# Key values taken out of the first values of the RWKV jobs, and gate pieces moved behind the merges

## What is computed

```python
def step(S, inp):                                  # one token, state S (64x64) of each of 16 heads
    r_t, w_t, k_t, v_t, kk_t, a_t = inp
    sa = jnp.einsum('bhvk,bhk->bhv', S, -kk_t)
    S = (S * w_t[:, :, None, :] + sa[..., None] * (kk_t * a_t)[:, :, None, :]
         + v_t[..., None] * k_t[:, :, None, :])
    y = jnp.einsum('bhvk,bhk->bhv', S, r_t) if emit else None
# run forwards and backwards, first over the 256 context tokens (state only), then over the 256 own tokens
g_rwkv, g_mla = jnp.split(jax.nn.sigmoid(p_gate + P['gate_b']), N_BRANCH, axis=-1)
merged = g_rwkv * (y_rwkv @ P['w_rwkv_proj']) + g_mla * (o @ P['w_mla_proj'])
```

## Time and profile before

| | |
|---|---|
| median of 3 runs | 3978.01 us (3964.2 to 3978.38) |
| the profiled execution: time, span | 3959.27 us, 3957.5 us |
| TensorE busy in the span | 3676.5 us (93%) |
| VectorE busy | 1319.2 us (33%) |
| ScalarE busy | 534.7 us (14%) |
| GpSimd busy | 162.4 us (4%) |
| mean granted clock of TensorE | 0.946 |

### The profile page before, as it was taken

The page is one execution under the profiler, slowest core; times in us unless marked ns, Lnnn a source line. Parts: engine busy times, 40 slices in busy tenths (PEclk is TensorE's granted clock), DMA queues, the critical chain, the costliest instruction groups (busy, mean ns, idle before and its releaser), DMA issues.

```text
span 3957.5 us, 43113 instructions
## 1 busy us (share of the span) xinstructions
PE 3676.5 (93%) x18466; PEld 2909.9 (74%) x18466; DVE 1319.2 (33%) x1920; ACT 534.7 (14%) x911; POOL 162.4 (4%) x166
## 2 busy tenths in 40 slices
PE   6999989978989869998999999999899979999979
PEld 2554545547768758887888888888788858888858
DVE  2388532235466530112321222000261261070260
ACT  1000002233333210110000000000101130101120
POOL 0020000000000000000000000000050000050000
PEclk8999999988888789999999999999899979999989
DMA  8989332012321144443444444444244303344303
GB/s 334 355 351 377 117 104 71 25 48 77 78 69 43 40 180 157 149 170 128 145 153 148 148 150 155 151 150 156 88 149 149 140 21 138 116 152 146 128 32 128
DMA packets 134889, 555.70 MB, mean 140 GB/s; under 512 B 57424, under 2 KB 62800, under 8 KB 73056
## 3 DMA queue, kind: packets, MB, share of 16 engines
q1 hardware_dynamic: 119392, 449.88, 32.6%
q10 hardware_dynamic: 15344, 103.57, 6.7%
HBM read 536.10 MB, written 17.30 MB: 140 GB/s over the span
## 4 chain that ended last, share of the span: by engine, by line
PE 59%; DVE 3%; ACT 1%; issue 1%; ACTq 0%; POOLq 0%; DVEq 0%
PE ps L433 56%; PE ps L2764 1%; PE ps L2525 0%; PE ps L2772 0%; PE ps L2520 0%; PE ps L463 0%; DVE arena L2821 0%; ACT arena L2899 0%; PE ps L2506 0%; DVE arena L2977 0%; PE ps L2773 0%; DVE arena L2286 0%; DVE arena L2960 0%; DVE arena L2741 0%; DVE arena L2295 0%
## 5 line engine op out<-in xcount | busy, mean ns | idle before, releaser
L433 PE MATMUL ps<-arena,ring 128*128 128x256 f32 (+3 forms) x11200 | 2583.2, 393 | 60.1 <-ACTq L2163 22.1
L433 PEld LDWEIGHTS ps<-arena,ring 128*128 128x128 f32 (+1 forms) x11200 | 2135.7, 191 | 504.1 <-issue 212.3
L764 DVE SCALAR_TENSOR_TENSOR arena<-arena,small 128x512 f32<-128x512 f32 x240 | 194.3, 809 | 24.0 <-DVE arena L764 9.5
L2269 DVE TENSOR_TENSOR arena<-ps,arena 128x1024 f32<-128x1024 f32 x12 | 14.3, 1222 | 394.9 <-ACT arena L2255 394.9
L2644 DVE SCALAR_TENSOR_TENSOR arena<-arena,col 128x255 f32<-128x255 f32 (+29 forms) x180 | 108.2, 601 | 6.4
L568 PE MATMUL ps<-arena 128*128 128x512 f32 (+1 forms) x224 | 90.1, 550 | 5.3 <-ACT arena L629 5.3
L2388 DVE TENSOR_TENSOR arena<-ps,arena 128x1024 f32<-128x1024 f32 x11 | 13.5, 1225 | 239.2 <-PE ps L433 239.0
L1529 PE MATMUL ps<-arena 128*128 128x256 f32 x320 | 87.4, 436 | 4.9 <-ACT arena L1739 4.9
L2652 POOL TENSOR_TENSOR arena<-arena 128x1024 f32<-128x1024 f32 x2 | 4.7, 2348 | 1994.8 <-ACT arena L2593 1994.8
L1971 DVE TENSOR_TENSOR arena<-arena 64x30 f32<-64x30 f32 (+14 forms) x240 | 83.8, 349 | 8.3
L2367 ACT ACT_TABLE_LOAD x11 | 14.1, 1283 | 535.0 <-DVE arena L2401 535.0
(11 more groups left out here) (417 smaller groups left out, 3135.8 us busy)
## 6 DMA issues: line engine op xcount, KB each, us to landing
ring<-in_weights SPq DMA_DIRECT2D x398, 1024.0 KB, 4.8
arena<-in_ada_late ACTq DMA_DIRECT2D x64, 1024.0 KB, 7.9
arena<-in_gates SPq DMA_DIRECT2D x56, 256.0 KB, 3.9
arena<-in_front ACTq DMA_DIRECT2D x8, 1024.0 KB, 9.1
arena<-in_x ACTq DMA_DIRECT2D x2, 2048.0 KB, 12.8
keep_g<-arena SPq DMA_DIRECT2D x14, 256.0 KB, 2.0
arena<-keep_g ACTq DMA_DIRECT2D x1, 3584.0 KB, 23.8
arena<-in_ctx ACTq DMA_DIRECT2D x1, 2048.0 KB, 23.6
```

The lines of the kernel that those rows point to most:

```text
L433: mm = M.matmul(o, ring[:, slot, k, c0:c0 + w], rhs, start=(kc == 0), stop=(kc == ktiles * WK - 1))
L764: ins = V.scalar_tensor_tensor(part[:, b], late[:, s, k], c, part[:, b], ALU.mult, ALU.add)
L2269: V.tensor_tensor(dst[:, 4 * b:4 * b + 4], ps[:, 4 * h:4 * h + 4, 0:T], spread(c[:, 4 * b:4 * b + 4], 4, T), ALU.mult).then_inc(dve_step.s ...
```

## The change

It does four things.

1. The product with `MR` leaves the first products. `key_values(n)` does it ahead of the own products of job n+1, 16 matmuls of 128 x 64 into a bank each for x = 0 and 1; ScalarE copies them to a new tile `Gv` (behind `turn_inverse`, `key_rates` and the gate copies), and the own products wait for both copies (`g_in`). What is left of the first products is `state_values`, 8 matmuls for each x with 64 rows each. The copy of the first values leaves ScalarE: VectorE adds state value and `Gv` (`first_values`, behind `key_factors(n+1)`, ahead of `substitute(n+1, 0..15)`).
2. ScalarE's `gate_copies(n, "own")` moves behind `turn_inverse(n)` and `key_rates(n+1)`.
3. The groups of jobs 1 to 3 that stood at "own" get the spots `LATER` and bank 5. The last piece of `STEPS` moves from "fin" to a new spot "z6", inside the merge of 64. In all, jobs 1 to 3 have none of their eight pieces ahead of the own products any more; the number of pieces is the same in each job.
4. SP loads the first group of job n before the substitution of job n is ready, not behind the unpacking. The tiles of the gate copies move (with waits for their stores in ScalarE's copies and, once, in VectorE's `key_factors`).

The diff, cut to its core:

```diff
+        Gv = view(RB + 13312, 2, 512)
...
-        gate_part = view(RB + 13312, 2, 512)
+        gate_part, gate_part_late = view(3072, 2, 512), view(RB + 21792, 512)
-        STEPS, LATER = ("z5", "x5", "x5", "fin"), ("fin", "fin", "u", "u")
-        GATE_GROUPS = [(0, 4, ("own",) * 4, "own"), (0, 5, ("own",) * 4, "own"), (0, 4, STEPS, "fin"), (0, 5, LATER, "u")]
-        GATE_GROUPS += [(n, *g) for n in range(1, 4) for g in ((4, ("own",) * 4, "own"), (4, STEPS, "fin"))]
+        STEPS, LATER = ("z5", "x5", "x5", "z6"), ("fin", "fin", "u", "u")
+        GATE_GROUPS = [(0, 4, ("own",) * 4, "own"), (0, 5, ("own",) * 4, "own")]
+        GATE_GROUPS += [(n, *g) for n in range(4) for g in ((4, STEPS, "fin"), (5, LATER, "u"))]
...
             return gate_w_late[:, k - 2]
+
+        def gate_copied(i):
+
+            return gate_part[:, i % 2] if i < CTX_GROUPS else gate_part_late
...
                 sp.wait_ge(gate_out.sem, i + 1)
-                sp.dma_start(A['keep_g'][:, i * 512:(i + 1) * 512], gate_part[:, i % 2])\
+                sp.dma_start(A['keep_g'][:, i * 512:(i + 1) * 512], gate_copied(i))\
                     .then_inc(gate_stored[i % 2].sem, 16)
...
                     sp.dma_start(gate_h_late, A['keep_h'][:, 0:2048].rearrange("p (c t) -> p c t", c=RC)).then_inc(gate_h_in.sem, 16)
-                for i in gates_by(n, "own")[n == 0:] if n < 4 else gates_of(n) if n < JOBS else ():
+                first = gates_by(n, "own") + gates_by(n, "fin") if n > 0 else gates_by(0, "own")[1:]
+                for i in first if n < JOBS else ():
                     load_gates(i)
...
-                if n < 4:
+                if n == 0:
                     for i in gates_by(n, "fin"):
...
+            def key_values(n):
+                emit = n >= 4
+                for x in range(2):
+                    p.wait_ge(ev['mr_in'], mr_count(n, 4 if emit else x + 1))
+                    p.wait_ge(ev['tok_in'], 4 * n + 2)
+                    for h in range(8):
+                        mm = M.matmul(ps[:, (4 if emit else 6) + x, h * 64:(h + 1) * 64], MR[:, x, h, 0],
+                                      vtok(n, x, h), start=True, stop=True)
+                    mm.then_inc(ev['g_mm'], 1)
+
             def gate_pieces(n, spot):
...
                     mm.then_inc(ev['z6_mm'], 1)
+                gate_pieces(n, "z6")
                 for x in range(2):
...
-            def first_products(n, x):
+            def state_values(n, x):
...
                 s, hf, q, i, b = job(n)
-                if x == 0:
-                    p.wait_ge(ev['mr_in'], mr_count(n, 4 if n >= 4 else 2))
-                    if n >= 4:
-                        p.wait_ge(ev['tr_in'], 2 * (n - 4) + 2)
+                if x == 0 and n >= 4:
+                    p.wait_ge(ev['tr_in'], 2 * (n - 4) + 2)
+                elif x == 0:
+                    p.wait_ge(ev['mr_in'], mr_count(n, 2))
                 t, st = slice(x * P, x * P + P), St[:, direction(n, x)]
                 for c in range(HF):
-                    o = [ps[:, 2 * x + e, c * 64:(c + 1) * 64] for e in range(2)]
-                    for e in range(2):
-                        M.matmul(o[e], AR[64 * e:64 * e + 64, b, c, 0, t], st[64 * e:64 * e + 64, hf * HF + c],
-                                 start=True, stop=False)
-                    for e in range(2):
-                        mm = M.matmul(o[e], MR[:, x, 4 * e + c, 0], vtok(n, x, 4 * e + c), start=False, stop=True)
+                    for e in (0, 64):
+                        mm = M.matmul(ps[:, 2 * x + e // 64, c * 64:(c + 1) * 64], AR[e:e + 64, b, c, 0, t],
+                                      st[e:e + 64, hf * HF + c], start=True, stop=True)
                 mm.then_inc(ev['u0_mm'], 1)
...
                     p.wait_ge(ev['p_in'], 2 * n + 3)
+                else:
+                    p.wait_ge(ev['g_in'], 2 * n + 2)
                 t, st = slice(x * P, x * P + P), St[:, direction(n, x)]
...
                     p.wait_ge(ev['dec_in'], n + 2)
-                    gate_pieces(n, "own")
-                    if n >= 4:
-                        p.wait_ge(ev['mr_in'], mr_count(n, 4))
-                    elif gates_by(n, "own"):
+                gate_pieces(n, "own")
+                key_values(n)
+                if more:
+                    p.wait_ge(ev['g_in'], 2 * n + 2)
+                    if gates_by(n, "own"):
                         p.wait_ge(gate_out.sem, gates_by(n, "own")[-1] + 1)
                     own_products(n + 1)
-                first_products(n, 0)
+                state_values(n, 0)
                 state_reads(n, 0)
...
                 gate_pieces(n, "z5")
-                first_products(n, 1)
+                state_values(n, 1)
                 merge_32_second(n)
...
-            def first_values(n, x):
-                a.wait_ge(ev['u0_mm'], 2 * n + x + 1)
-                S.copy(U0[:, x].rearrange("p (b t) -> p b t", b=2), ps[:, 2 * x:2 * x + 2, 0:256]).then_inc(ev['u0_in'], 1)
+            def key_values(n):
+                for x in range(2):
+                    a.wait_ge(ev['g_mm'], 2 * n + x + 1)
+                    S.copy(Gv[:, x], ps[:, (4 if n >= 4 else 6) + x, :]).then_inc(ev['g_in'], 1)
...
                 px = PX[:, n % 2]
-                first_values(n, 0)
                 reads_copy(n, 0)
...
                 S.copy(W5[96:128], w5[96:128]).then_inc(ev['z5_in'], 1)
-                first_values(n, 1)
                 a.wait_ge(ev['x5_mm'], n + 1)
...
                 for i in gates_by(n, act):
-                    if i >= 2:
-                        a.wait_ge(gate_stored[i % 2].sem, 16 * (i // 2))
+                    last = i - 2 if i < CTX_GROUPS else i - 1 if i > CTX_GROUPS else -1
+                    if last >= 0:
+                        a.wait_ge(gate_stored[last % 2].sem, 16 * (last // 2 + 1))
                     a.wait_ge(piece_mm.sem, 4 * i + 4)
-                    S.copy(gate_part[:, i % 2], ps[:, GATE_GROUPS[i][1], :]).then_inc(gate_out.sem, 1)
+                    S.copy(gate_copied(i), ps[:, GATE_GROUPS[i][1], :]).then_inc(gate_out.sem, 1)
...
                     decays(n + 1)
-                    gate_copies(n, "own")
                 turn_inverse(n)
...
                     key_rates(n + 1)
+                gate_copies(n, "own")
+                key_values(n)
                 merges(n)
...
+                    if n == 5:
+                        for stored in gate_stored:
+                            v.wait_ge(stored.sem, 16 * (CTX_GROUPS // 2))
...
                         ins.then_inc(ev['subst'], 1)
+
+            def first_values(n):
+                for x in range(2):
+                    v.wait_ge(ev['u0_mm'], 2 * n + x + 1)
+                    if x == 0:
+                        v.wait_ge(ev['g_in'], 2 * n + 2)
+                    V.tensor_tensor(U0[:, x].rearrange("p (b t) -> p b t", b=2), ps[:, 2 * x:2 * x + 2, 0:256],
+                                    Gv[:, x].rearrange("p (b t) -> p b t", b=2), ALU.add).then_inc(ev['u0_in'], 1)
...
                     key_factors(n + 1)
+                first_values(n)
                 if more:
...

```

More of the change, by code:

```diff
@@ L1241, in build_program @@
         L = {n: line(f"rw_{n}") for n in (
-            "w_mm a_mm tri_mm p_mm t_mm mr_mm tr_mm z5_mm x5_mm z6_mm fin_mm u0_mm u_mm s_mm sr_mm y_mm "
+            "w_mm a_mm tri_mm p_mm t_mm mr_mm tr_mm g_mm z5_mm x5_mm z6_mm fin_mm u0_mm u_mm s_mm sr_mm y_mm "
             "sig_in a_in dec_in kd_in ab_ready kt_ready r_ready p_in pk_out pk_in subst yt_in y_out unpacked "
-            "tok_in mr_in tr_in z5_in x5_in z6_in fin_in zero5 zero6 u0_in u_in s_in sr_in y_in "
+            "tok_in mr_in tr_in g_in z5_in x5_in z6_in fin_in zero5 zero6 u0_in u_in s_in sr_in y_in "
             "v_mm v_in sq_in ss_mm root_in inv_in kkb_mm kk_in ones_in").split()}
```

## The result

The changed kernel takes 3918.2 us (median of 4 runs, 3910.1 to 3919.6) against 3977.1 for the kernel before: a ratio of 0.9855, 95% interval 0.983 to 0.988. In a later comparison it took 3922.0 against 3965.4, ratio 0.9884 (0.9869 to 0.9899). So it is 43 to 59 us faster where 27 were forecast: the direction is right, the size is off by a factor of about two. Nearer to 43, if anything: three of the four runs of before in the first comparison lay at 3976 to 3978, while its medians in the four later ones, 58 runs in all, are 3964.8 to 3967.1.

The account below looks back on a forecast made before the run. Each job was taken as a ring from VectorE's substitution through factors, own products, packing, merges and state back to VectorE. Job terms summed to -27.1 us, giving 3932, plus 18.7 to the median: 3951 us, range 3932 to 3971.

Parts of the forecast that it names:

- allowance from one execution to the median: Whole kernel: 18.7 us between profiled execution and median of the runs before, added to the forecast 3932 to give 3951.
- x = 0 product: First product for x = 0, ahead of the merge: shortening it saves 4.6 us in job 4, 2.7 in jobs 5 and 6.
- x = 1 product: First product for x = 1, behind the merge: saves 3.0 us in jobs 0 to 3, 2.75 in 5, 4.65 in 4, 6, 7.
- Part a: Jobs 1 to 3: ScalarE's turn ahead of the gate copy brings unpacking and merge 6.15 us sooner in each.
- wait of 2 to 3 us at the merge: Jobs 1 to 3: TensorE gets a new wait of 2 to 3 us at the merge for SP's unpacking.
- Part c: Jobs 1 to 3: four gate pieces moved from 'own' to behind the merges cost 7.2 us a job at full clock.
- part b: All jobs: key product leaves the first products; key values ahead of own products take 3.7 us, 7.4 at half clock.
- More than that: Rival, 0.17: filled gap warms key values and own products in jobs 4 to 6, state values cost half; -42 us, about 3937.
- Half clock in the gap: Rival, 0.20: key values and state values run at half clock behind TensorE's gap, costing 18 us, leaving -9, 3969 us.
- gap: Experiments' theory: key values fill TensorE's idle time ahead of the own products, holding the clock; filler alone 10 to 20 us faster.
- The turn buys nothing: Rival, 0.06: something else holds the unpacking in jobs 1 to 3, so 6.15 us don't come; +18, leaving -9, 3969 us.
- slower: Rival, 0.07: light gap keeps the clock low through merges and moved pieces in jobs 1 to 3; +28, 4006 us.

Follow-up runs that it names:

- e5: Kernel before with only ScalarE's copy of the 'own' gate pieces moved behind the turn and the key rates: 3947.1 us against 3965.9, ratio 0.9952.
- e3: Changed kernel with the gate pieces of jobs 1 to 3 at their old spots, ScalarE's new order kept: 3899.0 us against 3964.8, ratio 0.9836.
- r2: Second run of e3's kernel, beside the changed kernel on the same chip: 3892.7 us against 3965.4 for the kernel before, ratio 0.9817.
- r1: Changed kernel run again unaltered for a second profile: 3922.0 us against 3965.4 for the kernel before, ratio 0.9884.
- e2: Changed kernel's pieces and orders, but the kernel before's first products, state and key matmuls pair by pair: 3970.8 us against 3964.8, ratio 1.0004.
- e1: Kernel before with each first product split into state, then key matmuls, at the old place: 3941.5 us against 3964.8, ratio 0.9943.
- e6: Changed kernel with the key values behind the own products, gap ahead of them empty: 3941.6 us against 3965.9 for the kernel before, ratio 0.9936.
- e4: Kernel before with 16 unread key-value matmuls as filler ahead of the own products in jobs 0 to 6: 3964.6 us against 3964.8, ratio 0.9997.
- e7: Changed kernel's pieces and orders, first products pair by pair, unread key matmuls filling the gap: 3979.9 us against 3965.9 for the kernel before, ratio 1.0022.
- e10: Kernel before with 16 unread 128 x 256 matmuls as heavy filler ahead of the own products in jobs 0 to 3: 3974.9 us against 3967.1, ratio 1.0015.
- e9: Changed kernel with old piece spots and ScalarE's old order, only the key values left: 3915.0 us against 3965.4 for the kernel before, ratio 0.9877.

## Why the prediction was off

**The sum by its steps.** The forecast was 3951 us, the median came out at 3918.2, 33 us below. The stage gives 31 of them (58.0 us gone in the profiles, not 27.1), and the longer part ahead of it takes 9 back. Another 10.5 are the allowance from one execution to the median: 18.7 us by three runs of before, 8.2 for the changed kernel, and 6 to 8 for before by the later medians. That allowance was put on the forecast as if it were a constant of the kernel. In the stage three blocks, predicted against measured in the two profiles of the changed kernel:

| | predicted | first profile | second profile |
|---|---|---|---|
| ahead of the merge (turn, own products late, x = 0 product) | -20.0 | -35.1 | -15.4 |
| merge to merge of 64 (x = 1 product) | -28.7 | -44.7 | -44.8 |
| from the merge of 64 on (pieces) | +21.6 | +21.8 | +21.7 |
| stage | -27.1 | -58.0 | -38.6 |

**Part a, right.** e5 measures it by itself: 19 us for three jobs, predicted 18.5. In the changed kernel the merge of jobs 1 to 3 comes 13.4, 14.4 and 14.6 us after the masks in the first profile and 14.4, 14.2 and 15.6 in the second, predicted 14.6. What the earlier trace rows say of the factor and the earlier trace rows of the unpacking was read correctly. The wait of 2 to 3 us at the merge was not: it is 0.3, 0 and 1.5 us, 0, 1.1 and 2.6 in the second profile, mostly because the own products come later and at half clock.

**Part c, right.** The moved pieces cost 21.8 and 21.7 us, predicted 21.6; e3's kernel gets them back and 7 more (29 us, r2 beside r1). What I called "the change's headline part, a and c together, is worth 3 us in all" is what e2 measures: no difference. (By the terms the 3 us are a loss, -18.5 + 21.6, though the sentence reads like a gain.) I didn't ask whether a needs c. It doesn't.

**Part b, the key values, the sizes that held.** 3.8 us at full clock and 7.1 at half (3.7 and 7.4 predicted), state values 1.1 and 2.0 (as taken), the hand-over 0.7. VectorE's add was never late: it ended 4.8 us ahead of the packed blocks in job 1, and 0.7 us or more ahead of them in every job of both profiles.

**The step that failed** is in part b: "Their saving for x = 1, always on TensorE's own path behind the merge: 3.0 us in job 0 and in jobs 1 to 3, 2.75 in job 5 (full clock), 4.65 in jobs 4, 6 and 7". It prices the product that goes, at the clock it had, and leaves everything between merge and merge of 64 at the clock that *it* had. That interval fell by 44.7 us and not 28.7. Taken apart in the timelines, summed over the jobs from the start of each group to the start of the next, the product itself fell from 39.9 us to 11.1 (11.3 in the second profile): 28.8, what was priced. The rest of the interval, pieces, merges and reads, was put at no change and fell from 91.4 us to 75.4 (75.1): 16 us, of them 10 in the pieces. TensorE did the same work there; it ran at half clock for much of the interval in six of the jobs before (16.6 to 17.6 us each) and now mostly at full: in job 1 the z5 piece gives 1.8 us and the x5 pieces 2.4. e1 and e6 show that the split does most of it, and e4, e7 and e10 that filling the gap in front doesn't do it without the split. e9, which has the key values and nothing else of the change, measures the whole of part b: 50 us, where its terms add up to 30. The term for the work that stays was put at nothing without a reason: its clock was taken from a profile in which the mixed product stood beside it.

**The term that isn't a constant.** Ahead of the merge the sum said -20.0. The two executions gave -35.1 and -15.4: in the one the key values of jobs 4 to 6 came at the full clock (masks to own products 10.5, 9.1, 9.1 us), in the other at half (13.1, 13.1, 13.0). I had half in job 4, full in 5 and 6, from one profile of before. A range with both clocks would have been the honest term. The first profile's -35.1, and with it a part of the size of the miss, is luck; the 16 us between the merges stand in both profiles.

**The rivals.** "More than that" (0.17, -42 us) has the nearest number, and for the most part not for its reason. Warm key values and own products in job 4 came in the first profile and not in the second, and the state values cost what I took, not half. Where the 16 us came, in the pieces, merges and reads between the merges, it had no term. (Its own terms add up to -41, and the range is widened at its low end by 4 us and not by the 14 that it names.) "Half clock in the gap" was half true: the key values of job 1 ran cold in both profiles (6.4 and 7.1 us for 3.7), and held the own products by some 2 us (factor at 983.91, own products at 985.75). By the rule of the Trainium skill cited with it ("TensorE: Matmul & The Clock Gate", Part 1) the products behind each gap start slow; the trace agrees for jobs 1 to 3 (5.6 to 7.1 us for the key values in the first profile, 4.8 to 7.1 in the second), and for jobs 4 to 7 only in the second profile (7.1 us each, 3.8 to 3.9 in the first). That sustained activity releases the slow clock is not what job 4 of before shows. TensorE works for 24.48 us without a wait, from the own products to the end of the second state reads, at half clock throughout (0.50):

```profile
1173.72:1198.20 24.48, 24.48 (x289) 21.81 (x290) 17.36 (x39) 4.87 (x11) 0.61 (x2) 0.50 0.20 36
```

(Columns as in the first rows above.) Here the measurement decides: an idle wait of 2.6 us stands ahead of this stretch and may have begun it, but no further one was needed to keep the clock down for 24 us, and that speaks against *gap* as the whole cause. "The turn buys nothing" and "slower" didn't occur; from the merge of 64 to `U` every job of both profiles took 9.3 us (7.4 in jobs 4 to 7), so the x5 pieces, or the m64 pieces in jobs 4 to 7, had brought the clock up by then.

**Left open.** Why mixed first products at full clock (job 1 of before had 0.91 there) leave half clock behind them, and the split ones mostly don't, isn't settled: the runs show that it is so in sum over the jobs, not in every job (first and second profile of job 1). Whether it is the alternation of 64 and 128 rows or the accumulation of both into one tile that matters wasn't tried, nor a filled gap with the split products behind it. What exactly the clock follows wasn't measured.

## What to carry to other kernels

When a change takes light work out of a stretch, price the rest of that stretch at both clocks, not at the one it had: here the neighbours gained 16 us beside the 29 of the part that went. Where two moves come in one change, ask of each whether it needs the other: here one call moved in ScalarE's order had the whole gain of the reordering (19 us), and the pieces that moved along cost 22 and gave nothing; without them the kernel is at 0.982 of before instead of 0.988. And where a stage flips between two clocks, one profile is a sample: two profiles of one kernel differed by 19 us in the stage.

## What the runs showed of the hardware

16 matmuls of 128 x 64 on all rows take 3.7 us at full clock and 7.1 at half; pair by pair with 64-row matmuls 8 and 8 take 3.8 us at full clock (job 5 of before, until the next group starts), in two groups 3.0 (job 4 of e1). TensorE worked 24.5 us without a wait over such small matmuls in job 4 of before and was granted half clock all the while (0.50); in job 1 of the changed kernel it was granted the full clock (1.00) from the merge to the merge of 64. Light filler in a gap changed the time by nothing (0.9997), heavy filler lifted the clock for the own products (1.16 us for 2.08), and that was gone behind the mixed products and a wait of 3.4 us. With the same program the same job ran its pieces in 1.99 us in one execution and 3.78 in another.
